# State-space decays summed on TensorE from fp32r high and low parts instead of float32

## The reference, cut to what matters

```
adt = (dt * a).reshape(b_, nc, L, G, R).transpose(0, 3, 4, 1, 2)
a_cs = jnp.cumsum(adt, axis=-1)
tri = jnp.tril(jnp.ones((L, L), dtype=bool))
diff = a_cs[..., :, None] - a_cs[..., None, :]
lmat = jnp.exp(jnp.where(tri, diff, -jnp.inf))
cb = jnp.einsum('bclgn,bcsgn->bcgls', cc, bc)
y_diag = jnp.einsum('bcgls,bgrcls,bcsgrp->bclgrp', cb, lmat, x)
```

## Time and profile before

| quantity | value |
|---|---|
| median of 3 runs | 1691.1 us (1690.8 to 1699.52) |
| span of the profiled execution | 1688.8 us |
| PE busy | 1654.1 us, 98% |
| DVE busy | 1179.2 us, 70% |
| ACT busy | 932.7 us, 55% |
| POOL busy | 49.4 us, 3% |

### The profile page before, as it was taken

One profiled execution on the slowest core, in us unless ns is written; L12 is line 12 of the kernel. 1 busy time (PEld: TensorE's weight loads), 2 busy tenths in 40 slices (PEclk: granted clock), 3 DMA queues, 4 the chain that ended last, 5 costly groups with the idle time before them and its releaser, 6 DMA issues.

```text
span 1688.8 us, 30601 instructions
## 1 busy us (share of the span) xinstructions
PE 1654.1 (98%) x10346; PEld 1473.7 (87%) x10346; DVE 1179.2 (70%) x1907; ACT 932.7 (55%) x1560; POOL 49.4 (3%) x44
## 2 busy tenths in 40 slices
PE   7999999999999999999989999999999999999998
PEld 6888898888898788879979999999999888888887
DVE  5555687597665655466664799989999856566664
ACT  6445545477555544456454444467777654545454
POOL 0000004000000000010010000110000000000000
PEclk9999999999999999999999999999999999999999
DMA  7555463334453655545354455544444466565553
GB/s 267 187 185 187 164 209 128 100 113 138 150 187 125 202 184 187 188 155 177 116 175 150 163 164 201 168 164 160 157 154 152 158 200 196 189 196 189 196 192 119
DMA packets 78813, 286.78 MB, mean 170 GB/s; under 512 B 8864, under 2 KB 9120, under 8 KB 78624
## 3 DMA queue, kind: packets, MB, share of 16 engines
q1 hardware_dynamic: 77888, 282.27, 50.4%
q0 software_dynamic: 864, 3.67, 0.6%
HBM read 284.86 MB, written 1.05 MB: 169 GB/s over the span
## 4 chain that ended last, share of the span: by engine, by line
PE 93%; DVE 4%; ACT 2%; issue 1%; DMA 0%; POOL 0%; ACTq 0%; DVEq 0%; POOLq 0%
PE ps L1776 29%; PE ps L1778 28%; PE ps L1777 28%; DVE w_low L1013 1%; PE ps L2344 1%; PE ps L2345 1%; PE ps L1791 1%; PE ps L1873 1%; ACT w_high L488 1%; DVE xT_low L1052 0%; PE ps L2309 0%; PE ps L2153 0%; PE ps L2015 0%; PE ps L2033 0%; PE ps L2172 0%
## 5 line engine op out<-in xcount | busy, mean ns | idle before, releaser
L1013 DVE TENSOR_TENSOR w_low<-ring,w_high 128x1024 fp32r<-128x1024 f32 x532 | 653.4, 1232 | 325.1 <-ACT w_high L488 323.2
L488 ACT ACTIVATE w_high<-ring 128x1024 fp32r<-128x1024 f32 x532 | 559.1, 1055 | 304.7 <-PE ps L1778 295.7
L1776 PE MATMUL ps<-xT_high,w_high 128*128 128x256 f32 x1600 | 460.8, 288 | 2.2 <-DVE xT_low L1052 2.2
L1777 PE MATMUL ps<-xT_high,w_low 128*128 128x256 f32 x1600 | 453.3, 283 | 0.0
L1778 PE MATMUL ps<-xT_low,w_high 128*128 128x256 f32 x1600 | 453.1, 283 | 0.0
L1776 PEld LDWEIGHTS ps<-xT_high,w_high 128*128 128x128 f32 x1600 | 307.1, 192 | 4.6 <-DVE w_low L1013 2.6
L1777 PEld LDWEIGHTS ps<-xT_high,w_low 128*128 128x128 f32 x1600 | 307.3, 192 | 0.7 <-issue 0.5
L1778 PEld LDWEIGHTS ps<-xT_low,w_high 128*128 128x128 f32 x1600 | 307.2, 192 | 0.0
L1776 PE MATMUL ps<-w_high,expert_w_high 128*128 128x512 f32 x512 | 199.5, 390 | 0.4 <-DVE expert_w_low L1739 0.4
L1778 PE MATMUL ps<-w_low,expert_w_high 128*128 128x512 f32 x512 | 199.3, 389 | 0.0
L1777 PE MATMUL ps<-w_high,expert_w_low 128*128 128x512 f32 x512 | 199.3, 389 | 0.0
(11 more groups left out here) (378 smaller groups left out, 2030.1 us busy)
## 6 DMA issues: line engine op xcount, KB each, us to landing
ring<-in_stream SPq DMA_DIRECT2D x532, 512.0 KB, 3.3
row_gain<-in_rows POOLq DMA_DIRECT2D x4, 512.0 KB, 4.5
h<-in_x SPq DMA_DIRECT2D x2, 512.0 KB, 5.5
mem_sb<-in_mem SPq DMA_DIRECT2D x1, 1024.0 KB, 10.3
keys_sb<-in_keys POOLq DMA_DIRECT2D x1, 1024.0 KB, 5.2
out<-result SPq DMA_DIRECT2D x2, 512.0 KB, 2.6
last_gain<-in_rows POOLq DMA_DIRECT2D x1, 512.0 KB, 4.4
cols<-in_cols SPq DMA_DIRECT2D x1, 78.5 KB, 3.4
```

What stands on the lines that cost most here:

```text
L488: act.activation(WH[:, n % SLOTS, :], RING[:, n % SLOTS, :], ACT.Copy).then_inc(w_high, 1)
L1013: dve.tensor_tensor(WL[:, n % SLOTS, :], RING[:, n % SLOTS, :], WH[:, n % SLOTS, :].bitcast(F32), ALU.subtract).then_inc(w_split, 1)
L1776: pe.matmul(out, high, w_hi, start=start, stop=False, skip_group_check=True)
L1777: pe.matmul(out, low, w_hi, start=False, stop=False, skip_group_check=True)
```

## The change

The step sizes are split by DVE into an fp32r high part and the rest, two operations of 128x32. POOL spreads both, so `adt` has two products of 128x2048 where it had one. PE sums both with an fp32r ones matrix, two fp32r matmuls for each bank in place of one float32 matmul. POOL now waits for the two parts (`adt_ok`), and `row_sums` for two counts a tile and for `ONES_R` (`masks_r`, made by DVE at line 1312, ahead of the scores' operations). The low part lies in the place of `tmp` and `attention_out` (81 KB), which are not in use here.

```diff
-    AU = sb("adt_upto", [P, 16, P], 113)
+    AUH = sb("adt_upto_high", [P, 16, P], 113, F32R)
+    AUL = sb("adt_upto_low", [P, 16, P], 81, F32R)
+    ADTH = sb("adt_high", [P, 32], 205.5, F32R)
+    ADTL = sb("adt_low", [P, 32], 205.75, F32R)
...
         def ssd():
-            pool.wait_ge(dt_d, 3)
+            pool.wait_ge(adt_ok, 2)
             pool.wait_ge(conv_done, 12)
 
             def adt(tt):
-                pool.tensor_tensor(AU[:], SS[:, 12, tt * 16:tt * 16 + 16].unsqueeze(2).to_broadcast([P, 16, P]),
-                                   UPTO[:].unsqueeze(1).to_broadcast([P, 16, P]), ALU.mult).then_inc(au_ok, 1)
+                for adt, upto in ((ADTH, AUH), (ADTL, AUL)):
+                    pool.tensor_tensor(upto[:], adt[:, tt * 16:tt * 16 + 16].bitcast(F32).unsqueeze(2).to_broadcast([P, 16, P]),
+                                       UPTO[:].unsqueeze(1).to_broadcast([P, 16, P]), ALU.mult).then_inc(au_ok, 1)
...
+        dve.wait_ge(dt_d, 3)
+        dve.tensor_copy(ADTH[:], SS[:, 12, :]).then_inc(adt_ok, 1)
+        dve.wait_ge(adt_ok, 1)
+        dve.tensor_tensor(ADTL[:], SS[:, 12, :], ADTH[:].bitcast(F32), ALU.subtract).then_inc(adt_ok, 1)
         conv(2, 2)
...
-            pe.wait_ge(au_ok, tt + 1)
+            pe.wait_ge(au_ok, 2 * tt + 2)
             pe.wait_ge(future_r, 2)
+            pe.wait_ge(masks_r, 2)
             for q in (2 * half, 2 * half + 1):
                 o = PS[:, 2048 + q * 512:2560 + q * 512]
-                pe.matmul(o, ONES[:], AU[:, 4 * q:4 * q + 4, :].rearrange("p h n -> p (h n)"),
+                pe.matmul(o, ONES_R[:], AUH[:, 4 * q:4 * q + 4, :].rearrange("p h n -> p (h n)"),
                           start=True, stop=False)
+                pe.matmul(o, ONES_R[:], AUL[:, 4 * q:4 * q + 4, :].rearrange("p h n -> p (h n)"),
+                          start=False, stop=False)
```

More of the change, by code:

```diff
@@ L347, in build @@
     final_ok = sem("final_ok")
-    future_r = sem("future_r_ok")
+    future_r, adt_ok = sem("future_r_ok"), sem("adt_split_ok")
     masks_r, sp_high, sp_low = sem("masks_r_ok"), sem("softplus_high_done"), sem("softplus_low_done")
```

## The result

The changed kernel takes 1705.7 us in the median of 10 runs (1700.8 to 1706.8), the kernel before 1695.7 us over 10 runs taken beside it (1690.4 to 1699.5). The ratio is 1.0056, with an interval of 1.0041 to 1.0071: slower, and above the top of my range, 1699.7 us. The slowest execution of the kernel before is still faster than the fastest of the changed one. The median of the kernel before is higher here than the 1691.1 us of the three runs first shown; its times lie in groups around 1691, 1695, 1696.6 and 1699.3 us, and the mean granted TensorE clock of an execution is 0.995 of full speed in the first group, 0.993 in the second and 0.990 in the last two. The changed kernel has two groups, 1701 to 1702 us (0.990) and 1705.5 to 1706.8 us (0.987).

The account below looks back on a forecast made before the run. PE was taken as the bound, 93% of the chain that ended last. Matmuls -3.2, stalls +1.9 and +5.2, clock +1.7 gave +5.6 us: span 1688.8 to 1694.4, plus 2.3 makes 1696.7 us, range 1687.7 to 1699.7.

Parts of the forecast that it names:

- The matmuls: On PE, a `row_sums` call falls from 2.18 to 1.4 us; the four calls save 3.2 us.
- The two small operations: On DVE, some 0.4 us with the wait between them, absorbed by 0.52 us of idle time; cost nothing.
- POOL against DVE, one after the other, in turns: A two-operand DVE operation from SBUF and a POOL product never run together; when both wait, they take turns.
- The second rival: DVE keeps its turn when its next instruction follows directly: stalls of 0.5 and 1.6 us, 1690.0 us; chance 0.17.
- the third rival: Clearly slower: POOL's product into fp32r takes longer than into float32; 1700.7 or 1698.4 us at 1 us more; chance 0.11.
- The first rival: The covers hold, nothing waits, only the 3.2 us saved are seen: 1687.9 us; chance 0.12.
- The first stall: PE waits 1.9 us before `xs_tokens(1)` for DVE's late `tokens_out(0)`, in the first tile.
- The second: PE waits 5.2 us before `within(0)` for DVE's `masked(0, 1)`, held up by POOL's second-tile products.
- The clock: PE's slowed clock behind the 5.2 us stall costs 1.7 us, nothing behind the 1.9; bounds 0 and 1.7 each.
- The base: Starting time of the kernel before: a span of 1688.8 us plus 2.3 by which the median stands above it.
- The sum for the stretch: Net change from matmuls, both stalls and clock: -3.2 + 1.9 + 5.2 + 1.7 = +5.6 us.

Follow-up runs that it names:

- e1: Changed kernel with one POOL product per tile, TensorE multiplying the high part twice; 1691.5 us, ratio 0.9978 to the kernel before.
- e2: Kernel before with a second, unread float32 POOL product behind each first one, PE waiting for both; 1702.3 us, ratio 1.0046 to the kernel before.
- e5: Changed kernel with 18 more fp32r matmuls of 128x512, sums unused, ahead of `within(0)`; 1696.3 us, ratio 1.0004 to the kernel before.
- e4: Changed kernel with the second product only in `adt(1)`, tile 0 multiplying the high part twice; 1700.5 us, ratio 1.0039 to the kernel before.
- e6: Changed kernel with POOL starting `adt(1)` only when `masked(0, 1)` is done; 1694.6 us, ratio 0.9995 to the kernel before.
- e10: e6 with both `tokens_out` copies and `panel(4)` ahead of the splits of steps 18 and 19 on DVE; 1691.6 us, ratio 0.9980 to the kernel before.

## Why the prediction was wrong

The mechanism was right. One term of the sum, the clock, was mis-sized, and the base on which the sum stands was low. By its own steps:

- **The matmuls**, 3.2 us: right. A call takes 1.38 us for the 1.4 forecast.
- **The two small operations**: right. Behind them DVE still sits idle 0.42 us for ACT's copy and 0.72 us for PE's running sums, and e1 has them and gains.
- **POOL against DVE, one after the other, in turns**: right in every row shown, four times at the second tile. The second rival, that DVE keeps its turn, is out: `panel(3)`'s copy starts 8.90 us behind the split of step 14, and not 5.63. Of the third rival only the sign is left: POOL's product into fp32r takes 3.61 us as before, and e2 shows the same 4.59 us in float32. The time is clearly slower, as that rival has it, but by the clock. The first rival, that the covers hold, fell with both waits.
- **The first stall**: 1.6 us for 1.9 forecast. **The second**: 4.4 for 5.2; the turns came without a gap as forecast, but the row of them, from the end of step 19's split (286.0) to the end of `masked(0, 1)` (307.65), is 21.6 us long and not 22.3.
- **The clock**: this is the step that failed. "I charge 1.7 us to the stall of 5.2 us", with 1.7 as the upper bound too. The trace has 8.3 + 3.2 - 6.0 = 5.5 us, and e5 gives 5.2 of it back by filling the wait. I had read the price from one place in one execution, where PE idled 2.64 us and was slow for some 3 us of work, and carried it over as if it were a price for each fall. In this stretch, with one trace each, it was 3.4 us behind a wait of 3.0 (e2), 5.0 behind 3.9 (e4) and 5.5 behind 4.4, and nothing behind 1.0 to 1.6. The length of the wait is not all that sets it: the same wait near 740 us lost twice the clock in the changed kernel's trace, and there 512-column matmuls follow, here the 64-column ones of `within(0)`. Which of these matters was not varied. The longest idle time in the rows was half of my stall, so 1.7 was no bound from above. The trace of the kernel before even had a dearer place, which I passed over. Behind waits of 2.60 and 2.19 us, in windows of PE:

```profile
864.00:866.00 2.00, 1.72 (x8) 0.60 1.00 426
866.00:868.00 2.00, 0.00 (x1) 0.50 0.77 311
868.00:870.00 2.00, 2.00 (x9) 0.50 0.75 250
870.00:872.00 2.00, 2.00 (x14) 0.70 0.20 59
```

The busy time lost there is 1.72 x 0.40 + 2.00 x 0.50 + 2.00 x 0.30 = 2.3 us.

- **The base**: 1688.8 + 2.3 us, low by 4.6 us, the largest single part of the miss of 9.0. Three runs were too few for times that lie in groups up to 5 us apart, and I hung the sum on the lowest group.

The sum for the stretch was +5.6 and is +8.3: 3.8 us more by the clock, 1.1 less by the two waits. That alone would have given some 1699 us. The median of the kernel before moved up by 4.6 us with more runs. The last 1.7 us are what the medians' 10.0 us have beyond the stretch; the profiled pair has its further 6.5 us at places that the change does not touch, where the clock falls in both kernels, for longer in the one trace than in the other. The fall near 740 us is short in the traces of the kernel before and five others, and long in those of the changed kernel and six others, so one trace of each kernel can't say whether the change makes them longer; that it does so by moving when they come was not tested.

## What to carry to other kernels

Before giving POOL another product, look at every two-input DVE operation around it, above all those that PE's next step waits for: here one more product of 3.6 us a tile on an idle POOL put nothing on PE's path by itself, and cost 6.0 us of waiting through DVE and 5.5 more by the clock. The cure was to start POOL's work behind the DVE operations that PE waits for (e6), and to move the copies that PE waits for ahead of the splits (e10). A wait of PE is to be priced with what its clock does behind it, from a row whose idle time is as long as the wait and which is followed by the same kind of work; if there is none, the price is open upward. And one execution gives one price of several: look at a second one. And when one copy on an in-order queue is moved ahead, look at the next one that the same engine owes.

## What the runs showed of the hardware

In every row shown POOL and DVE took turns at instruction boundaries when both wanted to read SBUF with two operands, also when each had its next instruction ready: 4.59 us for a POOL product of 3.61, 4.40 and 4.62 us for DVE operations of 1.2. The TensorE clock was at half behind every wait of 2.9 us or more in this stretch (2.9, 3.0, 3.9 and 4.4 us), and at full speed behind those of 1.6 us or less. Behind that of 4.4 us it stayed at half through 11 us in which PE was busy, 7.1 of them with matmuls of 64 columns. The Trainium skill (SBUF — State Buffer, Who interferes with whom) has the exclusion, that one of the two engines waits while the other reads, and the rows here agree (4.59 us for 3.61); who comes next is from the rows.
